# Grouping the attention of a two-layer encoder by four heads beside its query projection

## The reference, cut to what matters

```python
kv = rms_norm(h, kv_norm_w) @ w_kv                      # norm 2 below
q = (rms_norm(h, attn_norm_w[1]) @ w_q) * 64 ** -0.5    # norm 3: the same h, another gain
s = einsum(q, k_band) + bias                            # 16 heads, 4 chunks, 64 to 192 keys
m = maximum(max(s), sink)
p = exp(s - m) / (sum(exp(s - m)) + exp(sink - m))
h = h + concat(p @ v_band) @ w_o
# then norm 4, router, experts
```

## Time and profile before

| | us |
|---|---|
| median of 3 runs | 1628.02 (1627.79 to 1628.46) |
| the profiled execution, its time | 1626.98 |
| the profiled execution, its span | 1625.1 |
| TensorE busy | 1538.8 (95%) |
| VectorE busy | 1143.5 (70%) |
| ScalarE busy | 891.7 (55%) |
| GpSimd busy | 103.0 (6%) |
| stage: query projection | 520.4 to 548.3 |
| stage: attention | 548.9 to 598.2 |
| stage: output projection | 598.2 to 625.9 |
| stage: up to the first expert product | 625.9 to 655.4 |

### The profile page before, as it was taken

One profiled execution on the slowest core, in us unless ns is written; L12 is line 12 of the kernel. 1 busy time (PEld: TensorE's weight loads), 2 busy tenths in 40 slices (PEclk: granted clock), 3 DMA queues, 4 the chain that ended last, 5 costly groups with the idle time before them and its releaser, 6 DMA issues.

```text
span 1625.1 us, 22045 instructions
## 1 busy us (share of the span) xinstructions
PE 1538.8 (95%) x8769; PEld 1281.1 (79%) x8769; DVE 1143.5 (70%) x1001; ACT 891.7 (55%) x769; POOL 103.0 (6%) x66
## 2 busy tenths in 40 slices
PE   7889988999987887999999999999999999999997
PEld 7885984899976655788888888888888888888885
DVE  4565254544432453899899888888898889889895
ACT  4630122433421121577777777777777777777773
POOL 2330001000000000000000000000000000100100
PEclk9989889999998887999999999999999999999999
DMA  7432102655562206599999999999999999999992
GB/s 280 146 127 66 41 1 69 211 181 181 181 225 85 104 1 233 191 394 389 366 397 372 366 391 368 374 396 382 368 394 368 378 394 363 377 394 366 377 389 94
DMA packets 194028, 438.01 MB, mean 270 GB/s; under 512 B 5216, under 2 KB 28032, under 8 KB 193856
## 3 DMA queue, kind: packets, MB, share of 16 engines
q1 hardware_dynamic: 188944, 423.64, 70.8%
q0 software_dynamic: 2736, 9.31, 2.3%
q10 hardware_dynamic: 2304, 4.43, 0.8%
HBM read 429.48 MB, written 7.88 MB: 269 GB/s over the span
## 4 chain that ended last, share of the span: by engine, by line
PE 87%; DVE 7%; ACT 3%; issue 1%; DMA 1%; POOL 1%; DVEq 0%; POOLq 0%; ACTq 0%
PE bank L1404 23%; PE bank L1406 23%; PE bank L1405 23%; PE bank L1615 3%; PE bank L1732 2%; PE bank L1440 2%; PE bank L1875 1%; DVE weights_lo L1101 1%; DVE ws L930 1%; PE bank L1528 1%; PE bank L1545 1%; ACT qkv_hi L631 1%; PE bank L1474 1%; PE bank L1783 1%; PE bank L1749 1%
## 5 line engine op out<-in xcount | busy, mean ns | idle before, releaser
L1101 DVE TENSOR_TENSOR weights_lo<-weights,weights_hi 128x2048 fp32r<-128x2048 f32 (+1 forms) x398 | 825.6, 2117 | 153.1 <-ACT weights_hi L732 151.8
L732 ACT ACTIVATE weights_hi<-weights 128x2048 fp32r<-128x2048 f32 (+1 forms) x398 | 687.5, 1778 | 250.1 <-PE bank L1406 88.9
L1404 PE MATMUL bank<-weights_hi,expert_x_hi 128*128 128x512 f32 x896 | 354.9, 396 | 1.4 <-DVE expert_x_lo L1283 1.1
L1406 PE MATMUL bank<-weights_hi,expert_x_lo 128*128 128x512 f32 x896 | 349.4, 390 | 0.0
L1405 PE MATMUL bank<-weights_lo,expert_x_hi 128*128 128x512 f32 x896 | 349.2, 390 | 0.0
L1404 PE MATMUL bank<-weights_hi,hidden_hi 128*128 128x512 f32 x536 | 211.2, 394 | 6.2 <-DVE weights_lo L1101 4.1
L1405 PE MATMUL bank<-weights_lo,hidden_hi 128*128 128x512 f32 x536 | 209.4, 391 | 0.0
L1406 PE MATMUL bank<-weights_hi,hidden_lo 128*128 128x512 f32 x536 | 209.2, 390 | 0.0
L1406 PEld LDWEIGHTS bank<-weights_hi,expert_x_lo 128*128 128x128 f32 x896 | 168.2, 188 | 36.4
L1404 PEld LDWEIGHTS bank<-weights_hi,expert_x_hi 128*128 128x128 f32 x896 | 168.3, 188 | 35.4 <-DVE expert_x_lo L1283 1.2
L1405 PEld LDWEIGHTS bank<-weights_lo,expert_x_hi 128*128 128x128 f32 x896 | 168.4, 188 | 33.4
(11 more groups left out here) (286 smaller groups left out, 1561.8 us busy)
## 6 DMA issues: line engine op xcount, KB each, us to landing
weights<-in_moe_w_down SPq DMA_DIRECT2D x56, 2048.0 KB, 9.5
weights<-in_moe_w_up SPq DMA_DIRECT2D x56, 2048.0 KB, 9.6
weights<-in_moe_w_gate SPq DMA_DIRECT2D x55, 2048.0 KB, 9.5
weights<-in_a_w_in SPq DMA_DIRECT2D x8, 2048.0 KB, 8.9
weights<-in_ffn_w_up SPq DMA_DIRECT2D x11, 1024.0 KB, 5.3
weights<-in_ffn_w_gate SPq DMA_DIRECT2D x11, 1024.0 KB, 5.4
weights<-in_ffn_w_down SPq DMA_DIRECT2D x11, 1024.0 KB, 4.9
weights<-in_a_w_out SPq DMA_DIRECT2D x2, 2048.0 KB, 8.3
```

Source lines behind the costliest of these rows:

```text
L732: act.activation(whi[k][:, j * n:(j + 1) * n], slot[k][:, j * n:(j + 1) * n], ACT.Copy).then_inc(w_hi[k], 1)
L1101: dve.tensor_tensor(wlo[k][:, c], slot[k][:, c], whi[k][:, c].bitcast(F32), ALU.subtract).then_inc(w_lo[k], 1)
L1404: pe.matmul(dst, ah, bh, start=start, stop=False, skip_group_check=True)
L1406: return pe.matmul(dst, al, bh, start=False, stop=stop, skip_group_check=True)
```

## The change

- Norms 2 and 3 share one set of squares and roots (`rstd_of`).
- The attention goes by groups `g` of four query heads (two pairs) which share one key and value head, all four chunks of a group together. The queries of a group are one pair of column blocks. TensorE's order is written out: query 0, 1, scores 0, query 2, scores 1, values 0, query 3, scores 2, values 1, scores 3, values 2, a part of the projection, values 3, the rest of it.
- Bias, sink and maximum are one VectorE operation for each pair and chunk, `tensor_tensor_reduce`, eight for a group. The exponential takes the negated maximum as its bias and gives the sum itself, also eight for a group. The division is four operations for a group.
- The heads go into a buffer `oT` of their own, by one copy for each group. The output projection (`merge`) keeps four banks open at once: six of the eight products of each bank after the heads of groups 0 to 2, the last two of each after group 3.

```diff
+        def rstd_of(k):
+            return k if k < 3 else k - 1
...
-        sc = [view(ws, 9216 + 2048 * k, PAIRS, T) for k in range(2)]
+        sc = [view(ws, 9216 + 2048 * k, 2 * NC, T) for k in range(2)]
+        oT = view(ws, 16384, KT, T)
...
+        score_at = [(0, 0), (0, 128), (1, 0), (2, 0)]
...
-            for k in range(1, 5):
+            for k in (1, 2, 4):
                 norm_rstd(k)
...
-            squares(3)
...
-            for g in range(4):
+            def queries(g):
                 act.wait_ge(s_qmm, g + 1)
                 act.activation(qT2[:, 2 * g:2 * g + 2, :], ...
...
+            def exps(g):
+                b = g % 2
+                act.wait_ge(s_sub, g + 1)
+                for n in range(NC):
+                    k0, k1 = max(0, n - 2) * C, (n + 1) * C
+                    for j in range(2):
+                        r = 2 * n + j
+                        a = act.activation(sc[b][:, r, k0:k1], sc[b][:, r, k0:k1], ACT.Exp, bias=nmx[b][:, r:r + 1],
+                                           accum_out=den[b][:, r:r + 1])
+                a.then_inc(s_exp, 1)
+                act.activation(esk[b], esk[b], ACT.Exp).then_inc(s_esk, 1)
+
+            queries(0)
+            queries(1)
             exps(0)
+            queries(2)
+            for g in range(PAIRS // 2):
+                for n in range(NC):
+                    m = 4 * g + n
                     act.wait_ge(s_pt, m + 1)
...
+                if g == 0:
+                    queries(3)
+                if g < 3:
+                    exps(g + 1)
...
+            for k in range(2):
+                link(dve.memset(sc[k][:, 6:8, 0:C], 0.0))
+
+            def masked_scores(g):
+                b = g % 2
+                if g >= 2:
+                    dve.wait_ge(s_pt, 4 * (g - 1))
+                for n in range(NC):
+                    k0, k1 = max(0, n - 2) * C, (n + 1) * C
+                    L, b0 = k1 - k0, (2 * C if n == 0 else C if n == 1 else 0)
+                    dve.wait_ge(s_sc, 4 * g + max(n, 1) + 1)
+                    for j in range(2):
+                        r, c0 = 2 * n + j, score_at[n][1] + j * L
+                        i_ = dve.tensor_tensor_reduce(out=sc[b][:, r, k0:k1], in0=bank[score_at[n][0]][:, c0:c0 + L],
+                                                      in1=bias[:, 2 * g + j, b0:b0 + L], scale=1.0,
+                                                      scalar=sink[:, 2 * g + j:2 * g + j + 1], op0=ALU.add, op1=ALU.max,
+                                                      accum_out=mxa[b][:, r:r + 1])
                     i_.then_inc(s_scb, 1)
+                dve.wait_ge(s_scb, 4 * g + 4)
+                link(dve.tensor_scalar(nmx[b], mxa[b], -1.0, None, ALU.mult))
+                dve.tensor_tensor(esk[b].rearrange("p (n j) -> p n j", j=2), nmx[b].rearrange("p (n j) -> p n j", j=2),
+                                  many(sink[:, 2 * g:2 * g + 2], NC), ALU.add).then_inc(s_sub, 1)
+
+            def weights(g):
+                b = g % 2
+                dve.wait_ge(s_exp, g + 1)
+                dve.wait_ge(s_esk, g + 1)
+                link(dve.tensor_tensor(den[b], den[b], esk[b], ALU.add))
+                link(dve.reciprocal(rden[b], den[b]))
+                for n in range(NC):
+                    k0, k1 = max(0, n - 2) * C, (n + 1) * C
+                    s_ = sc[b][:, 2 * n:2 * n + 2, k0:k1]
+                    dve.tensor_tensor(s_, s_, wide(rden[b][:, 2 * n:2 * n + 2], k1 - k0), ALU.mult).then_inc(s_p, 1)
+
+            def heads_out(g):
+                dve.wait_ge(s_pv, g + 1)
+                dve.tensor_copy(oT[:, 2 * g:2 * g + 2, :], view(bank[5], 0, 2, T)).then_inc(s_oT2, 1)
+
+            for g in range(4):
+                masked_scores(g)
+                if g:
+                    heads_out(g - 1)
+                weights(g)
+            heads_out(3)
...
-                add_h(t, s_aw, 0, (0, 1, 2, 5), 8)
+                add_h(t, s_aw, 0, (0, 1, 2, 3), 8)
...
+            def scores(g):
+                pe.wait_ge(s_qT, g + 1)
+                for n in range(NC):
+                    k0, k1 = max(0, n - 2) * C, (n + 1) * C
+                    L, (b, c0) = k1 - k0, score_at[n]
+                    if g and n != 1:
+                        pe.wait_ge(s_scb, 4 * (g - 1) + max(n, 1) + 1)
                     for j in range(2):
...
+            def merge(kts, first, last):
+                for t in range(NT):
+                    for q in range(2):
+                        if first:
+                            pe.wait_ge(loaded[q], 16 * (PRE_A[q] + 2))
+                        for kt in kts:
+                            m = pe.matmul(bank[2 * t + q][:, :], oT[:, kt, t * P:(t + 1) * P], g8[q][:, kt, :],
+                                          start=first and kt == kts[0], stop=last and kt == kts[-1],
+                                          skip_group_check=True)
+                        if last:
+                            m.then_inc(s_aw, 1)
+
+            query(0)
+            query(1)
+            pe.wait_ge(s_bias, 4)
+            pe.wait_ge(s_kT, 2)
             scores(0)
+            query(2)
+            scores(1)
+            values(0)
+            query(3)
+            scores(2)
+            values(1)
+            scores(3)
+            values(2)
+            pe.wait_ge(s_scb, 16)
+            pe.wait_ge(s_qT, 4)
+            pe.wait_ge(s_oT2, 3)
+            merge(range(6), True, False)
+            values(3)
             pe.wait_ge(s_oT2, 4)
-            pe.wait_ge(s_scb, 16)
-            for t in range(NT):
-                project(t, (0, 1), (PRE_A[0] + 2, PRE_A[1] + 2), ((0, 1), (2, 5))[t], s_aw)
+            merge(range(6, 8), False, True)
```

More of the change, by code:

```diff
@@ L275, in trunk @@
         sink = view(sm, 344, PAIRS)
-        mxa = view(sm, 352, PAIRS)
-        den = view(sm, 368, PAIRS)
-        esk = view(sm, 376, PAIRS)
-        rden = view(sm, 384, PAIRS)
+        mxa, nmx, den, esk, rden = ([view(sm, 24 + 16 * a + 8 * k, 2 * NC) for k in range(2)] for a in range(5))
         relb = view(sm, 392, QH)
@@ L507, in norm_rstd @@
             def norm_rstd(k):
+                k = rstd_of(k)
                 for t in range(NT):
@@ L887, in norm_x @@
                     dve.wait_ge(s_row[k % 2], 16 * (k // 2 + 1))
-                dve.wait_ge(s_rstd, 2 * k + t + 1)
-                dve.scalar_tensor_tensor(out=xn[:, t, :], in0=h[:, t, :], scalar=rs[:, k, t:t + 1],
+                r = rstd_of(k)
+                dve.wait_ge(s_rstd, 2 * r + t + 1)
+                dve.scalar_tensor_tensor(out=xn[:, t, :], in0=h[:, t, :], scalar=rs[:, r, t:t + 1],
                                          in1=rows[k % 2][:, :], op0=ALU.mult, op1=ALU.mult).then_inc(s_xn, 1)
@@ L1722, in _ @@
             pe.wait_ge(s_vS, 1)
-            for c in range(2):
-                k = 1 + c
-                pe.wait_ge(loaded[k], 16 * (PRE_A[k] + 1))
-                for j in range(4):
-                    m_ = 4 * c + j
-                    g = m_ // 2
-                    if g >= 2 and m_ % 2 == 0:
-                        pe.wait_ge(s_qT, g - 1)
-                    for kt in range(KT):
-                        m = pe.matmul(bank[3 + g % 2][:, (m_ % 2) * T:(m_ % 2 + 1) * T],
-                                      g8[k][:, kt, j * P:(j + 1) * P], xt[:, kt, :], start=kt == 0, stop=kt == KT - 1)
-                    if m_ % 2:
-                        m.then_inc(s_qmm, 1)
@@ L1736, in _, with query @@
-            pe.wait_ge(s_qT, 4)
-            pe.wait_ge(s_bias, 4)
-            pe.wait_ge(s_kT, 2)
-            def scores(n):
-                k0, k1 = max(0, n - 2) * C, (n + 1) * C
-                for g in range(4):
-                    if n:
-                        pe.wait_ge(s_scb, 4 * (n - 1) + g + 1)
+            def query(g):
+                k = 1 + g // 2
+                if g % 2 == 0:
+                    pe.wait_ge(loaded[k], 16 * (PRE_A[k] + 1))
+                if g >= 2:
+                    pe.wait_ge(s_qT, g - 1)
+                for j in range(2):
+                    c = slice((2 * (g % 2) + j) * P, (2 * (g % 2) + j + 1) * P)
+                    for kt in range(KT):
+                        m = pe.matmul(bank[3 + g % 2][:, j * T:(j + 1) * T], g8[k][:, kt, c], xt[:, kt, :],
+                                      start=kt == 0, stop=kt == KT - 1)
+                m.then_inc(s_qmm, 1)
@@ L1752, in scores, with values @@
                     m.then_inc(s_sc, 1)
-            def values(n):
-                nk = 1 if n < 2 else 2
-                w = C if n % 2 == 0 else P
-                pe.wait_ge(s_p, n + 1)
-                if n >= 2:
-                    pe.wait_ge(s_oT2, n - 1)
-                for g in range(4):
-                    m_ = 4 * n + g
+            def values(g):
+                for n in range(NC):
+                    m_ = 4 * g + n
+                    nk, w = 1 if n < 2 else 2, C if n % 2 == 0 else P
+                    pe.wait_ge(s_p, m_ + 1)
```

(17 more changed lines are left out.)

59 lines of the change are left out of this document (5 added, 54 removed).

## The result

The changed kernel took **1618.2 us** (median of 4 runs, 1616.3 to 1620.3) beside 1628.2 us for the kernel before on the same chip: ratio 0.9931, 95% interval 0.9913 to 0.9948. That is 10.0 us less, where 4.1 were forecast. The time lies at the lower edge of the range 1618 to 1630 and the direction is right, but the gain is 5.9 us larger than the sum gave, so at least one of the terms is wrong, and the experiments had to say which.

What follows compares the result with a forecast made beforehand. Before an untouched, TensorE-bound expert loop, TensorE's projections and attention, with softmax waits and low clock, were taken as the bound. Terms -1.7 (root), -5.7 (stretch), +3.3 (tail) gave -4.1 us: 1623.9 us, own range 1622 to 1626, wide range 1618 to 1630.

Steps and rivals of the forecast that it cites:

- The root: Before the query projection: one root for norms 2 and 3 removes a wait at the bias copy, -1.7 us, bounds 1.2 to 4.4.
- rival 1: Bias-copy pause gets too short for the clock to fall: 2.7 us more gained, about 1621 us; chance 0.24.
- The stretch: First query product to output projection's end: terms sum to 99.8 us against 105.5, so -5.7.
- clock, extra: Half-rate starts behind pauses, query products to projection's end: 2 us taken, range 0 to 10, about 1.7 each.
- Wait (a): Ahead of values 1: group 1's exponentials stand behind query 3's copy on ScalarE, a TensorE pause of 3.1 us.
- Wait (b): Group 2's exponentials wait for ScalarE's last copy of group 1, leaving 1.5 us beyond scores 3.
- Both (c): The projection's first part waits for group 2's heads copy, its last quarter for group 3's: 0.9 us each.
- The new operations: Attention softmax: eight joined VectorE operations 3 us a group, hidden; eight exponentials with accumulator reads 3.6 us, charged in the waits.
- Rival 3: VectorE's new joined operation costs 1.25 us instead of 0.37, making attention 14.5 us late, 1638 us; chance 0.10.
- Rival 4: ScalarE becomes attention's chain, reads not overlapped and copies delayed, two waits 2 us longer each: 1627.5 us; chance 0.08.
- Rival 2: Value products leave query 3, scores 3 and both projection parts starting at half clock: surcharge 6 to 7, 1628 us; chance 0.16.
- The tail: Behind the projection: late up weights (+3.2 us), which cover a later router product, cost 3.3 us together, bounds 1 to 5.5.

Runs made afterwards that it cites:

- e3: Changed kernel with group 1's exponentials ahead of query 3's copy on ScalarE, not behind it: 1612.2 us, 0.9901 of the kernel before.
- e4: Changed kernel with every joined VectorE operation done twice, the second into spare space: 1618.3 us, 0.9931 of the kernel before.
- e6a: Changed kernel with the projection's up half first and the first up load issued ahead of the gate load: 1617.1 us, 0.9933 of the kernel before.
- e6c: Changed kernel with VectorE's remainders of the first chunk and of the up tile moved later: 1615.2 us, 0.9913 of the kernel before.
- e11: Changed kernel with twelve unread filler products in TensorE's 2.7 us pause ahead of value products 1: 1615.2 us, 0.9922 of the kernel before.
- e13: Changed kernel with six unread filler products in TensorE's 2.7 us pause ahead of value products 1: 1613.3 us, 0.9905 of the kernel before.
- e14: Kernel before with unread filler products sized to TensorE's three long attention pauses: 1628.8 us, ratio 0.9996.
- e16: Kernel before, its chunk order and two roots kept, with the changed kernel's joined softmax operations: 1627.3 against 1628.8 us, ratio 0.9992.
- e8: Changed kernel with subtraction and sum as separate VectorE operations and four plain exponentials a group: 1619.2 us, 0.9931 of the kernel before.
- e15: Changed kernel with six filler products ahead of value products 1 and two ahead of the projection's first part: 1614.3 us, 0.9908 of the kernel before.
- e2: Changed kernel with squares and roots for norms 2 and 3 made twice again: 1622.8 us, 0.9964 of the kernel before.
- e9: Changed kernel with exponentials ahead of query 3's copy and VectorE's two blocks of remainders later: 1608.1 us, 0.9867 of the kernel before.
- e10: Changed kernel with exponentials ahead of query 3's copy, VectorE's remainders later and up weights first: 1610.0 us, 0.9884 of the kernel before.

## Why the prediction was wrong in size

**The root** was the right mechanism: the wait was 1.7 us and 1.8 went. The term was mis-sized by the clock, which the forecast held at its old low stretch. One root alone measured 2.8. In the profiles of e3, e4, e6a, e6c, e11 and e13 it was 4.5 (32.9 from root to query, the clock at 1.00 throughout), which is rival 1's case with the 2.7 us that it named. In the other seven profiles with this head the clock fell. Whether it falls there is open from one execution to the next.

**The stretch was the wrong step**: -9.9 and not -5.7. By its terms, each from its start to the start of what follows:

| term | forecast | measured |
|---|---|---|
| query products | 27.9 | 28.2 |
| scores | 8.4 | 9.6 |
| transposes and value products | 27.4 | 25.5 |
| clock, extra | 2 | in the rows above |
| projection | 27.7 | 27.8 |
| waits | 6.4 | 2.7 + 0.0 + 1.0 + 0.8 = 4.5 |
| sum | 99.8 | 95.6 |

The step that failed is "Transposes and value products keep count and shape: 27.4" together with "Part of the 27.4 above was already at half clock, so I take 2". Four groups at full clock, of the same count and shape, take 4 x 5.6 = 22.4 us (e3, e13). The 27.4 thus held 5.0 us of half clock, and 2 were laid on top: 7.0. The changed kernel paid 3.0 in value products 1 and 1.1 in scores 3, 4.1 in all, and filling the pause gave that back, less 0.5 of new wait. A second error had the opposite sign: the forecast priced one fall at 1.7 us, from 3.4 us of low clock, while the one behind the long pause lasted 11 us and cost 4.1. A duration read at half clock was carried as if it belonged to the operation. The range for the clock, "0 to 10", went only up from 27.4: the floor of the term, five under it, was never taken, although the row had its clock beside it.

**The waits** were too dear by 1.9. Wait (a) measured 2.7 for 3.1. Wait (b), 1.5 forecast, was nothing: value products 1 at half clock lasted long enough to cover it. In the run with six fillers, where they were at full clock, 0.5 us of it appeared. Both (c) were right (0.9 each, measured 1.0 and 0.8).

**What set the kernel before** was read as "waits for maximum, exponential and division" plus the low clock, as if both could be won separately. e14 shows that they were one thing: its clock can be raised without a gain, since VectorE's and ScalarE's chain stood behind. e16 shows the converse, a lighter VectorE, with more work on ScalarE in exchange, without a gain. The new order is what works, because query products 2 and 3 and three quarters of the projection lie over that chain. The stretch held 49.9 us of attention and waits before and holds 39.6 now, against 30.8 us of it at full clock and without waits (22.4 and four times 2.1). Whether the kernel before would gain from the filler and the new operations together was not tried.

**The new operations** went as forecast: 0.21, 0.27 and 0.34 us from start to start for VectorE's at 64, 128 and 192 columns, 2.5 us for eight (3 taken), 3.2 us for eight exponentials (3.6 taken), their accumulator reads hidden. By the Trainium skill (VectorE: DVE Perf Modes, "The TRN2 errata") an operation out of PSUM costs 120 cycles and its columns at 0.96 GHz, an estimate of 0.19, 0.26 and 0.33 us; the trace agrees within 0.02 from start to start, while the durations recorded are longer, 0.28 to 0.42, and overlap. Rival 3 (1.25 us each) is refuted, and e4 shows that twice the price would not have decided anything. Rival 4 did not come. Rival 2 did not come in the changed kernel's profile, where both parts of the projection ran at full clock; in e4, e6a, e6c, e8, e11 and e15 one part had a fall, at 1.5 to 1.7 us each.

**The tail** was forecast at +3.3 and measured +3.1, the late up weights at 12.2 us for 11.7. Its mechanism held: the router's product ended 17.2 us behind the projection (17.5 forecast) and the up remainders 18.7 (18.2), and the load alone taken away gave little, as "covered by the late load with 0.7 us to spare" says: in e6a the router's product is what the arithmetic waits for, at 17.7, and in e15, where that product ended at 15.5, the arithmetic still waited for the remainders until 18.4. What the forecast did not see is that both holds come from VectorE's order and go together when its two blocks of remainders stand later (e6c, arithmetic at 15.4): the end of the load matters only because its remainders stand ahead of the router's arithmetic.

## What to carry to other kernels

A TensorE duration is two numbers, the work and the clock it ran at: bring each term to full clock first, and put the clock in as one term of its own, tied to the pauses that remain. A pause of 2.7 us cost 6.8 (e3), and more than half of the loss lay not in the pause but behind it; filling it with useless products won 3.6 (e13). But ask first whether another engine's chain lies underneath: in the kernel before the same filler brought nothing. And when a transfer is late, look at what stands queued behind the work on it: moving two blocks of 4.5 us on VectorE that nothing needed yet out of the router's way gave 3.0 us by the medians (e6c), issuing the transfer earlier nothing clear of the noise (e6a).

## What the runs showed of the hardware that was not expected

The granted clock fell to half behind pauses as short as 0.8 to 1.0 us: ahead of a part of the projection in e4, e6a, e6c, e8, e11 and e15, and in e2 and e14 at the query products (some 3.4 us long, 1.5 to 1.7 us of loss each). It did not fall behind the same pauses in the changed kernel, e3, e9, e10 and e13. What decides between the two was not found.

A value product whose two parts have 128 and 64 rows costs 0.13 us a record at full clock (16 records in 2.12 us in e14), one whose parts both have 128 rows 0.046 (16 in 0.73): chunk 2's products cost almost three times chunk 3's for less work. The cause was not looked for.
